# First weight half in two transfers, first pass block by block, first squares later, zeros multiplied until the tokens land

## What is computed

```python
def first_block(x, mix_pre_g, w_in, b_forget, ...):
    h = rmsnorm(x, mix_pre_g[l])      # x * rsqrt(mean(x*x) + eps) * g
    proj = h @ w_in[l]                # 1024 x 7176
    u, v_s, q, k, v_a, g_a, g_b, f_logit = jnp.split(proj, IN_SPLITS, axis=-1)
    y_a = spatial_gating(jax.nn.gelu(u), jax.nn.gelu(v_s), ...)
    y_b = forgetting_attention(q, k, v_a, f_logit, b_forget[l])
...
def ec_moe(h, router_w, w_gu, w_down):      # end of the second block
    logits = jnp.einsum('bnd,de->bne', h, router_w)
    aff = jax.nn.softmax(logits, axis=-1)
    gates, idx = lax.top_k(jnp.swapaxes(aff, 1, 2), cap)
    ...
```

## Time and profile before

| | |
|---|---|
| median of 3 runs | 1509.07 us (1507.6 to 1509.88) |
| the profiled execution | 1508.42 us, span 1506.6 us |
| busy: TensorE, weight loads | 1227.1 us (81%), 716.0 us (48%) |
| busy: VectorE, ScalarE, GpSimd | 406.2 us (27%), 307.2 us (20%), 31.0 us (2%) |
| mean granted TensorE clock | 0.873 of full speed |
| transfers | 500.91 MB, mean 332 GB/s |

### The profile page before, as it was taken

One profiled execution on the slowest core, in us unless ns is written; L12 is line 12 of the kernel. 1 busy time (PEld: TensorE's weight loads), 2 busy tenths in 40 slices (PEclk: granted clock), 3 DMA queues, 4 the chain that ended last, 5 costly groups with the idle time before them and its releaser, 6 DMA issues.

```text
span 1506.6 us, 16246 instructions
## 1 busy us (share of the span) xinstructions
PE 1227.1 (81%) x6957; PEld 716.0 (48%) x6957; DVE 406.2 (27%) x610; ACT 307.2 (20%) x431; POOL 31.0 (2%) x33
## 2 busy tenths in 40 slices
PE   8999999999999999985776766766758657767676
PEld 7888788888878566431231331321313313213222
DVE  5756455675356754100000000000000000000001
ACT  5544544444364544000000000000000000000001
POOL 1000000000030100000000000000000000000000
PEclk9999999999999999888778777768777886777799
DMA  9744435655544378999999999999999999999996
GB/s 340 261 169 173 161 112 180 207 172 210 186 163 112 112 285 338 424 427 427 427 425 428 428 428 428 428 428 428 427 428 428 427 428 427 428 427 428 427 427 289
DMA packets 85332, 500.91 MB, mean 332 GB/s; under 512 B 4975, under 2 KB 30005, under 8 KB 60581
## 3 DMA queue, kind: packets, MB, share of 16 engines
q1 hardware_dynamic: 84068, 495.60, 81.3%
q0 software_dynamic: 1216, 4.63, 0.9%
HBM read 499.16 MB, written 1.05 MB: 332 GB/s over the span
## 4 chain that ended last, share of the span: by engine, by line
PE 52%; DMA 44%; DVE 2%; ACT 1%; issue 1%; SPq 0%; POOL 0%; POOLq 0%; DVEq 0%; ACTq 0%
DMA arena<-in_expert_w_gu_dram 34%; PE psA L635 11%; DMA arena<-in_expert_w_down_dram 10%; PE psB L1297 5%; PE psB L1250 5%; PE psB L861 4%; PE psB L1207 4%; PE psA L674 4%; PE psB L674 3%; PE psA L678 2%; PE psA L1021 2%; PE psB L678 2%; PE psA L872 1%; PE psA L646 1%; PE psA L1086 1%; PE psB L1130 1%
## 5 line engine op out<-in xcount | busy, mean ns | idle before, releaser
L1250 PE MATMUL psB<-arena,x_res 128*32 128x512 f32 x2048 | 325.2, 769 | 197.1 <-DMA arena<-in_expert_w_gu_dram 197.0
L1250 PEld LDWEIGHTS psB<-arena,x_res 128*32 128x32 f32 x2048 | 63.4, 126 | 428.0 <-DMA arena<-in_expert_w_gu_dram 304.5
L1786 DVE TENSOR_TENSOR split_r<-arena,split_r 128x2048 fp32r<-128x2048 f32 x75 | 171.6, 2290 | 119.5 <-ACT split_r L1341 119.3
L1686 ACT ACTIVATE x_res<-psB 128x512 f32<-128x512 f32 x16 | 9.6, 597 | 838.8 <-PE psB L1250 838.8
L1341 ACT CAST split_r<-arena 128x2048 fp32r<-128x2048 f32 x77 | 146.8, 1911 | 107.8 <-PE psA L635 56.6
L635 PE MATMUL psA<-split_r,hT_r 128*128 128x512 f32 x720 | 167.0, 391 | 1.6 <-issue 1.0
L1297 PE MATMUL psB<-arena 128*32 128x512 f32 x1008 | 142.7, 721 | 10.6 <-DMA arena<-in_expert_w_down_dram 10.4
L635 PEld LDWEIGHTS psA<-split_r,hT_r 128*128 128x128 f32 x720 | 134.0, 188 | 30.3 <-issue 2.9
L1207 PE MATMUL psB<-sb_b,arena 128*128 (+1 forms) x512 | 105.3, 384 | 11.4 <-ACT arena L1688 11.3
L1207 PEld LDWEIGHTS psB<-sb_b,arena 128*128 128x128 f32 x512 | 103.0, 311 | 17.1 <-issue 13.5
L2310 DVE TENSOR_TENSOR x_res<-x_res,psB 128x512 f32<-128x512 f32 x16 | 16.4, 1026 | 280.0 <-ACT x_res L1686 280.0
(11 more groups left out here) (391 smaller groups left out, 1065.8 us busy)
## 6 DMA issues: line engine op xcount, KB each, us to landing
arena<-in_expert_w_gu_dram SPq DMA_DIRECT2D x128, 2048.0 KB, 35.4
arena<-in_expert_w_down_dram SPq DMA_DIRECT2D x62, 2048.0 KB, 36.0
arena<-in_w_in_dram SPq DMA_DIRECT2D x36, 1024.0 KB, 7.6
arena<-in_w_gate_dram SPq DMA_DIRECT2D x11, 1024.0 KB, 5.3
arena<-in_w_up_dram SPq DMA_DIRECT2D x11, 1024.0 KB, 8.2
arena<-in_w_down_dram SPq DMA_DIRECT2D x10, 1024.0 KB, 6.0
arena<-in_w_out_dram SPq DMA_DIRECT2D x6, 1024.0 KB, 5.5
arena<-in_ca_wkv_dram SPq DMA_DIRECT2D x4, 1024.0 KB, 6.3
```

The costliest lines, as they stand in the source:

```text
L1250: ins = pe.matmul(psB[32 * j:32 * j + 32, o, :], XC[:, k, :], w[4 * o + j], start=(k == 0), stop=(k == GU_SLOTS - 1), skip_group_check=True)
L1786: v.tensor_tensor(W_LO[n % 2].rearrange("p (k n) -> p k n", **shape), view, W_HI[n % 2].bitcast(F32).rearrange("p (k n) -> p k n", **shape ...
```

## The change

Four things at the start, and one renaming near the router.

1. The first transfer of vs0 (1 MB, blocks 0 to 3) becomes two: blocks 0 and 1, then blocks 2 and 3. VectorE rounds the first two, ScalarE the other two.
2. The first pass over vs0's first piece goes block by block, both token tiles for each block, with waits for each block's parts (first_pass).
3. ScalarE squares both token tiles, after it has rounded vs0's second half. VectorE makes the means after its low parts of vs0. Before, tile 0 was squared first thing on ScalarE and tile 1 on VectorE.
4. TensorE multiplies zeros (warm_up, from a tile that VectorE has cleared) eight times before the gains land and eight times after their transpose. The three products of keep_warm there go, and the two behind the tokens' transposes shrink from 512 to 128 columns.

```diff
@@ -498,6 +498,10 @@
                     else:
                         after_slot(sp, last)
                 for b, (dst, src) in enumerate(plan[i]):
+                    if i + b == 0:
+                        q = KT // 4
+                        sp.dma_start(dst[:, 0:q, :], src[:, 0:q, :]).then_inc(sig("first_quarter_loaded"), 16)
+                        dst, src = dst[:, q:, :], src[:, q:, :]
                     sp.dma_start(dst, src).then_inc(sig("first_half_loaded") if i + b == 0 else loaded_sem(i), 16)
 
             load(0)
@@ -623,11 +627,25 @@
 
                     yield j, xs[1 if j == 1 else 0], w, wait_x
 
+            def first_pass(pair):
+
+                h = KT // 2
+                w = W_HI[0].rearrange("p (k n) -> p k n", k=h)
+                for k in range(h):
+                    pe.wait_ge(sig("xh_ready"), k // 2 + 1)
+                    pe.wait_ge(*((sig("first_cast"), 1) if k < h // 2 else (sig("hi_ready"), 1)))
+                    for t in range(TT):
+                        pe.matmul(psA[:, 2 * pair + t, :], HTS[0][:, k, t * P:(t + 1) * P], w[:, k, :], start=(k == 0), stop=False)
+
             def tok_major_split(pair, name, tag=None, rows=(0, 1)):
 
                 h = KT // 2
                 for b in rows:
+                    if name == "vs0" and b == 0:
+                        first_pass(pair)
                     for j, x, w, wait_x in passes(name, b, HTS, tag):
+                        if name == "vs0" and b == 0 and j == 0:
+                            continue
                         for t in range(TT):
                             for k in range(h):
                                 if t == 0:
@@ -720,13 +738,20 @@
                     if k % 2 == 1 and t == 1:
                         ins.then_inc(sig("turned"), 1)
 
+            def warm_up(n):
+
+                for _ in range(n):
+                    pe.matmul(psA[:, 1, 0:TOK], c_pair[:, 0:P], c_pair[:, :], start=True, stop=True)
+
+            pe.wait_ge(sig("pair_zeroed"), 1)
+            warm_up(8)
             pe.wait_ge(sig("ident_vecs_loaded"), 16 * 2)
             pe.transpose(psA[:, 0, 0:NROW], VROWS, C("ident", NROW, NROW)).then_inc(sig("cols_tr"), 1)
-            keep_warm(psA[:, 1, 0:P], 3, ident)
+            warm_up(8)
 
 
             transposes("n1", X)
-            keep_warm(psA[:, 1, :], 2, X[:, 0, 0:NC])
+            keep_warm(psA[:, 1, 0:P], 2, X[:, 0, 0:P])
             pe.wait_ge(sig("cols_ready"), 1)
             tok_major_split(0, "vs0", tag="n1")
             tok_major_split(1, "vs1")
@@ -1332,10 +1357,7 @@
 
                 for n, view in pieces[name] if b is None else pieces[name][b:b + 1]:
                     i = where[name]
-                    if n == 0:
-                        act.wait_ge(sig("first_half_loaded"), 16)
-                    else:
-                        act.wait_ge(loaded_sem(i), loaded_no(i))
+                    act.wait_ge(loaded_sem(i), loaded_no(i))
                     if n >= 2:
                         act.wait_ge(sig("piece_used"), n - 1)
                     a.copy(W_HI[n % 2].rearrange("p (k n) -> p k n", k=view.shape[1]), view).then_inc(sig("hi_ready"), 1)
@@ -1355,13 +1377,16 @@
                 ins.then_inc(sig("squares"), 1)
 
 
-            act.wait_ge(sig("x0_loaded"), 16)
-            square("n1", X[:, 0, :])
             act.wait_ge(sig("cols_ready"), 1)
             operand_hi("n1", ROW["mix_pre_g"], banks=(0, 1))
-            split_hi("vs0", 0)
+            act.wait_ge(sig("first_half_loaded"), 16)
+            a.copy(W_HI[0].rearrange("p (k n) -> p k n", k=KT // 2)[:, KT // 4:, :],
+                   pieces["vs0"][0][1][:, KT // 4:, :]).then_inc(sig("hi_ready"), 1)
             operand_hi("n1", ROW["mix_pre_g"], banks=(2, 3))
             split_hi("vs0", 1)
+            for t in range(TT):
+                ins = a.activation(XN[:, t, :], X[:, t, :], ACT.Square, accum_out=SS[:, t:t + 1])
+            ins.then_inc(sig("squares"), 1)
 
             def from_pair(c, name, dst, func, signal):
 
@@ -1813,21 +1838,23 @@
                 ins.then_inc(sig(done_name), 1)
                 dve.wait_ge(sig(done_name), 1)
 
-            v.memset(c_pair[:, :].bitcast(F32), 0.0)
+            v.memset(c_pair[:, :].bitcast(F32), 0.0).then_inc(sig("pair_zeroed"), 1)
             v.memset(m_pair[:, :].bitcast(F32), 0.0)
             link(v.memset(GP[:, :], 0.0))
 
             dve.wait_ge(sig("cols_tr"), 1)
             v.tensor_copy(cols[:, :], psA[:, 0, 0:NROW]).then_inc(sig("cols_ready"), 1)
             dve.wait_ge(sig("cols_ready"), 1)
-            dve.wait_ge(sig("x1_loaded"), 16)
-            link(v.tensor_tensor_reduce(XN[:, 1, :], X[:, 1, :], X[:, 1, :], 1.0, 0.0, ALU.mult, ALU.add, SS[:, 1:2]))
-            dve.wait_ge(sig("squares"), 1)
-            v.tensor_scalar(VV[:, 0:2], SS[:, 0:2], 1.0 / D, EPS, ALU.mult, ALU.add).then_inc(sig("mean_ready"), 1)
+            dve.wait_ge(sig("first_quarter_loaded"), 16)
+            v.tensor_copy(W_HI[0].rearrange("p (k n) -> p k n", k=KT // 2)[:, 0:KT // 4, :],
+                          pieces["vs0"][0][1][:, 0:KT // 4, :]).then_inc(sig("first_cast"), 1)
             operand_lo("n1", ROW["mix_pre_g"], banks=(0, 1))
+            dve.wait_ge(sig("first_cast"), 1)
             split_lo("vs0", 0)
             operand_lo("n1", ROW["mix_pre_g"], banks=(2, 3))
             split_lo("vs0", 1)
+            dve.wait_ge(sig("squares"), 1)
+            v.tensor_scalar(VV[:, 0:2], SS[:, 0:2], 1.0 / D, EPS, ALU.mult, ALU.add).then_inc(sig("mean_ready"), 1)
             dve.wait_ge(sig("root_ready"), 1)
             for t in range(TT):
                 v.tensor_scalar(DG[:, t, :], ident, R1[:, t:t + 1], None, ALU.mult).then_inc(sig("rows_normed"), 1)
```

Near the router, the signals aff_ready, aff_tr and picks_mm become further counts of lg_ready and router_mm, raised by the same instructions and awaited at the same places:

```diff
-            pe.wait_ge(sig("aff_ready"), 1)
+            pe.wait_ge(sig("lg_ready"), 3)
...
-            ins.then_inc(sig("aff_tr"), 1)
+            ins.then_inc(sig("router_mm"), 1)
...
-            dve.wait_ge(sig("picks_mm"), 2)
+            dve.wait_ge(sig("router_mm"), 5)
```

More of the change, by code:

```diff
@@ L1195, in _ @@
                 ins = pe.transpose(psB[:, 2, t * NE:(t + 1) * NE], TKW[:, t * P:(t + 1) * P], C("ident", NE, NE))
-            ins.then_inc(sig("picks_mm"), 1)
+            ins.then_inc(sig("router_mm"), 1)
             keep_warm(psB[:, 3, 0:P], 1)
@@ L1200, in _ @@
             pe.matmul(psB[:, 1, NE:2 * NE], C("ones"), MKT[:, 0, :], start=True, stop=False)
-            pe.matmul(psB[:, 1, NE:2 * NE], C("le"), MKT[:, 1, :], start=False, stop=True).then_inc(sig("picks_mm"), 1)
+            pe.matmul(psB[:, 1, NE:2 * NE], C("le"), MKT[:, 1, :], start=False, stop=True).then_inc(sig("router_mm"), 1)
             def gather(c0, bank=3, ks=range(KT)):
@@ L2251, in _ @@
             link(v.reciprocal(T_a[:, 4:6], T_b[:, 0:2]))
-            v.tensor_tensor(AFF, AFF, T_a[:, 4:6].rearrange("p (t a) -> p t a", a=1).to_broadcast([P, TT, NE]), ALU.mult).then_inc(sig("aff_ready"), 1)
-            dve.wait_ge(sig("aff_tr"), 1)
+            v.tensor_tensor(AFF, AFF, T_a[:, 4:6].rearrange("p (t a) -> p t a", a=1).to_broadcast([P, TT, NE]), ALU.mult).then_inc(sig("lg_ready"), 1)
+            dve.wait_ge(sig("router_mm"), 3)
             src = psB[0:NE, 1, 0:TOK]
@@ L2263, in _ @@
             ins.then_inc(sig("picks_ready"), 1)
-            dve.wait_ge(sig("picks_mm"), 1)
+            dve.wait_ge(sig("router_mm"), 4)
             v.tensor_scalar(MKT.rearrange("p t e -> p (t e)"), psB[:, 2, 0:2 * NE], 0.0, None, ALU.is_lt).then_inc(sig("picks_ready"), 1)
             dve.wait_ge(sig("picks_ready"), 2)
-            dve.wait_ge(sig("picks_mm"), 2)
+            dve.wait_ge(sig("router_mm"), 5)
             link(v.tensor_tensor(POST.rearrange("p t e -> p (t e)"), psB[:, 1, 0:2 * NE], MKT.rearrange("p t e -> p (t e)"), ALU.mult))
```

## The result

The changed kernel takes 1511.31 us in the median of 16 runs (1508.12 to 1512.85), the kernel before 1508.38 us in the median of 16 (1506.32 to 1509.88). The ratio is 1.0022, with a 95% interval of 1.0015 to 1.0028. The change makes the kernel slower, by 0.2% in the first comparison and 0.1% in the second. The forecast was 1512.0, slower by 3.0 us.

A forecast was written before the change was run, and what follows sets the result against it. TensorE was taken as the chain, its delay before the experts moving the end equally: +1.3 (late gates) +1.7 (clock) = +3.0 us, the 1.9 us start gain already inside, so 1512.0 us; range 1507.0 to 1515.0.

The forecast's parts named there:

- the first term: Late root delays eight small transfers, so TensorE waits for the split gate weights and the gate product starts 1.3 us later.
- The second term: TensorE's clock falls to half for 3.4 us behind its idle before the gate product: 1.7 us, bounds 0 and 2.6.
- Zeros: Zeros on TensorE from 1.2 us raise its clock before 5.4; ScalarE's first operand starts near 7.2 instead of 7.91.
- a rival's price: Activation table load before the late square, 1.28 us, in the case of still later gates: 1514 us, chance 0.17.
- Quarters and blocks: First weight half in two transfers, rounded by two engines, first pass by blocks: passes end at 31.6, 1.9 us sooner.
- The small transfers: Eight transfers behind GpSimd's root issue from 17.8 or 17.9, 5.4 us later; the last lands at 33.65.
- rival A: Small transfers issued late are served faster and catch up; with a shift under 2.4 us, 1507.2 us. Chance 0.13.
- The gate product: TensorE wants the gates at 31.6, gets them at 34.6: idle 3.0 us, product starts 1.3 us later.
- The clock behind the idle: Granted clock 0.50 for 3.4 us behind TensorE's idle before the gate product, costing 1.7 us.
- a sign of being wrong: The prediction is wrong if the clock stays at 1.00 behind TensorE's idle before the gate product.
- B: Gates late by 1.3 us but TensorE's clock holds behind the idle: 1510.4 us. Chance 0.20.

The follow-up runs named there:

- the second: The changed kernel timed and profiled once more, nothing altered: 1510.19 us against 1507.92 for the kernel before, ratio 1.0010.
- queue: Changed kernel with GpSimd's root behind the issues of the eight small transfers instead of in front: 1507.54 us, ratio 0.9998.
- mean_later: Kernel before with only VectorE's means of the first norm moved behind its low parts of vs0: 1511.93 us, ratio 1.0032.
- after: First profile of the changed kernel, of its fastest execution (1508.12 us); median 1511.31 us, ratio 1.0022 to the kernel before.
- table: Changed kernel plus one tiny ScalarE square at the very start, so the activation table loads before the tokens land: 1509.71 us, ratio 1.0009.
- zeros: Kernel before with part 4 alone (zeros multiplied early, short products behind the transposes): 1507.82 us, ratio 1.0007.
- table_filled: Changed kernel with the early table load and 16 products of zeros on TensorE before its wait for the gates: 1508.31 us, ratio 1.0004.
- both: Changed kernel with GpSimd's root behind the small transfers' issues and the activation table loaded early: 1507.13 us, ratio 0.9996.
- squares_back: Changed kernel with part 3 undone (squares first on ScalarE and VectorE, means right behind): 1506.59 us, ratio 0.9995.
- back_filled: Changed kernel with part 3 undone and eight warm products in TensorE's wait near 187 us: 1505.41 us, ratio 0.9982.
- part3: Kernel before with the whole of part 3 alone (both squares late on ScalarE, means behind VectorE's low parts): 1511.18 us, ratio 1.0023.
- halves: Changed kernel without parts 3 and 4, leaving quarter transfers, shared rounding and the pass by blocks: 1507.20 us, ratio 0.9995.

## Why the prediction was right

The mechanism of the first term, the late gates, was right and shown from both sides: with the queue's order changed the loss goes (queue), and with the means alone moved it appears in the kernel before (mean_later). The second term, the clock, was seen in neither profile of the changed kernel. The sizes, step by step:

*Zeros.* Transposes at 0.11 apart: so in the first profile (from 5.64, not 5.4), not in the second, which took 3.67 us for the sixteen. Of the nine profiles with zeros five have all sixteen at full pace (after, queue, table, zeros, table_filled), in three the pace rises while they run (both, squares_back, back_filled), and in one it doesn't. The reading behind this term, "at 1.2 GHz until about 8 us", was made from the pace alone; the profile's granted clock is 1.00 all through these stretches, in the kernel before too, and nothing here explains that. That this brings ScalarE's first operand to 7.2: wrong. It came at 8.79, mostly for a term missing from the sum: the activation table's load, 1.28 us, was on no path before and moved behind the wait, which itself ended at 7.50. I had it as a rival's price ahead of the square; it stands ahead of the copies. There is no second load before the squares. That agrees with what I drew from the Trainium skill, "ScalarE: Activation LUTs", section "Table sets: the hidden batching unit", by which cheap functions such as copy are in every set; its list doesn't name the square.

*Quarters and blocks.* VectorE's rounding took 0.69 (0.75 taken), ScalarE's 1.06 (1.0). The gain of 1.9 us stood in no profile of the changed kernel: passes ended at 34.2 and 33.4 instead of 31.6. It stood in "both" (31.5). What ate it is the table load in each of the two profiles, with the half clock from 12 us on in the first profile and the slow transposes in the second (ScalarE's wait for them ended at 8.34, not 7.50).

*The small transfers.* Forecast: issued from 17.9, 5.4 later, landed at 33.65. Measured: from 18.35, 5.9 later, landed near 34.45; the second time the wait for them ended at 34.77. Their pace held (11.1 and 10.6 us from issue to landing, 10.8 before), so rival A is out.

*The gate product.* Forecast 1.3 us later, after 3.0 us of idle. Measured 2.15 and 2.4 later, after 1.28 and 2.33 us of idle. This is the mis-sized term, and it is the landing's: 0.8 and 1.1 us later than forecast. Of the 0.8, 0.5 was there at the issue, because VectorE's low parts, which stand in front of the means, waited for the later operands (11.40 for the low weights in place of 10.6, by the chain), and 0.3 is the longer way to landing.

*The clock behind the idle.* Forecast 1.7 us. It can happen: "table" and "part3" show it, 1.6 us each between the gate product's start and u0's. But in the two profiles of the changed kernel the clock held at 1.00, which the prediction had named as a sign of being wrong. The idle was shorter there than forecast, but its length alone doesn't decide: the clock fell behind 2.84 and 1.99 us and held behind 2.33, 1.86 and 1.28. The wait near 187 us says the same. It is 2.07 or 2.08 us long in all twelve profiles in which it isn't filled; half clock began at it or within 1.5 us after it in eight, and in four (the changed kernel's first, both, zeros, table_filled) the clock held. How often it falls in the changed kernel's other 25 executions isn't known; the medians (2.9 and 2.3 us) leave 0 to 0.8 us for it on top of the late gates.

So the sum of +3.0 was made of 1.3 and 1.7, and the measured +2.9 and +2.3 of 2.2 to 2.4 and, in the first, a rest of at most 0.8. Part of the agreement in the total is luck: two wrong sizes made up for each other. Of the rivals, B (late gates, clock holds) describes both profiles best, with a larger delay than I gave it.

## What to carry to other kernels

An instruction off the critical path can stand in a queue in front of transfers that aren't: before moving it, read what its queue issues behind it, and follow those transfers to who waits for them and with how much to spare (here 4.2 us of spare against a shift of 5.9). When an engine's first instruction changes, look where its table load goes; one tiny instruction at the start hides it. A gain in front of a late event is worth nothing until that event is early, and a clock raised before there is work for it can be down again when the work comes (zeros). Take a second profile of the same kernel before you explain a clock level in the first.

## What the runs showed of the hardware that was not expected

In two versions (changed, zeros) TensorE's clock fell at 12 us, 6 to 7 us after the first transpose at full pace, behind a stretch of waits (1.64 busy in 3.40 us, or nothing in 3.10), and stayed at half for 3.4 us. The same kernel has such a stretch at 12 us in one execution and at 191 in the next, with no difference in the program; each is worth 1.6 to 1.7 us when no later wait absorbs it. The tokens' landing also moved, with the first transposes between 5.0 and 6.2 us. Both may be a good part of the 3 to 5 us between the executions of one kernel; that was not shown, and what chooses the place of the half clock stays open.

GpSimd's root on 128x2 took 1.00 us in squares_back in place of 0.70, and 1.00 in halves and 1.20 in back_filled:

```profile
8.21 1.00 POOL L1734 TENSOR_TENSOR st<-st,power 128x2 f32<-128x2 f32 x1 [7.10 <-DVE st L1850]
```

VectorE was rounding its quarter just then (7.96 to 8.65), and so it was in the other two (8.62 to 9.31 and 8.54 to 9.23). The Trainium skill, "GPSIMD Engine Reference", section "1. Specifications", lists GpSimd's SBUF interfaces as shared with VectorE, with contention from VectorE's two-port modes and its instructions with two SBUF inputs. The times would fit that, but no row shows which mode this rounding runs in, and no run here takes one away from the other; it costs nothing in this place.
